# A hybrid block's front stage re-ordered: gate tiles by kind, four of them ahead of the merging of the inverses, spatial gate inside the first chunk, two groups of the recurrence alternating

## The chip, the cores and the metric

The kernel runs on one core of one Trainium2 chip. The metric is the device time of one execution in microseconds (us), here the median of three.

The engines are named as in the profile: PE (TensorE) does the matmuls, PEld its weight loads; DVE (VectorE) and ACT (ScalarE) work elementwise; POOL (GpSimd) and SP (SyncE) only issue transfers here. Every engine runs its own instructions in program order and waits on semaphores (`wait_ge`).

## What is computed

256 tokens, width 1024, fp32. One projection `z = RMSNorm(x) @ W_in` feeds two mixers, which are gated, added and projected out; a top-4-of-32 expert FFN follows.

```python
z_a, u_raw, v_raw, gate_logits = jnp.split(z, ...)
# yA: delta-rule state, 16 heads x 64, over time (in chunks of 64 in the kernel)
sa = einsum('bhij,bhj->bhi', state, -kk_t)
state = state * w_t + sa * (kk_t * a_t) + v_t * k_t
y_t = einsum('bhij,bhj->bhi', state, r_t)
# yB: inside 128-frame chunks
s = einsum('gij,bcjgd->bcigd', tril(ws), LN(gelu(v_raw))) + b_spatial
y_b = gelu(u_raw) * s
g_a, g_b = split(sigmoid(gate_logits + b_gate), 2)
x = x + (g_a * y_a + g_b * y_b) @ w_out
x = x + moe_ffn(rms_norm(x))      # 32 experts: w_gate_up (1024 x 2048), w_down (1024 x 1024) each
return rms_norm(x)
```

## The kernel before, in words

The order of the work is written out by hand, one program for each engine. The tokens are turned so that features lie on partitions; 256 tokens are the moving operand.

The front stage has these parts, in PE's order:

1. The projections of the recurrence's columns, eight pairs of 64-wide heads at a time (`products`, line 1115, makes the 64x64 blocks of each chunk).
2. The values of the spatial gate, `value_chunk`, into PSUM banks 0 to 3, which ACT empties with a gelu (`v_out`).
3. 24 **gate tiles** (`tile`, line 1178): each is eight 128x128 by 128x256 products of `w_in` with the tokens into one half bank. Eight are `u` (gelu), eight are the merge gate `b` and eight the merge gate `a` (sigmoid). They alternate between banks 0 and 1, so tile t waits until ACT has emptied tile t-2 (`f_out`). Their weights come by SP in 1 MB loads of two tiles.
4. **The inverses.** Each chunk needs the inverse of a 64x64 triangular matrix for each head. DVE inverts the 32x32 diagonal blocks on 128 lanes (31 steps of two instructions, lines 806 to 811) after ACT has sent them through memory into that layout (`scr_a`, `al`). ACT sends the result back through memory (`scr_x`, then four loads into `GB`), DVE turns it (`x1_ready`, line 820), and PE merges the blocks in two passes of 32x32 products: `with_x11` (line 1190) and `with_x22` (line 1198).
5. The **spatial gate**: eight pairs of 128x128 products (`spatial`, line 1206); DVE adds the bias and multiplies (lines 841 to 844).
6. **The recurrence**, four chunks q. It is made of groups of 16 products of 64x64 (for each of the eight c, the two half-partitions hh): `rows_of_values`, `rows_of_state`, `solved`, `state_of_values`, `state_of_solved`, `outputs_of_values`, and in `outputs` one group of the state and one of the solved rows. Between them stand `variances`, `spread_deviation` and, in three gaps for each chunk (`fill`, table `FILL`), the 16 tiles b and a. A tile a comes with `gate_lora` (bank 2).
7. The output projection `project_out` (line 1355), router, and then the experts.

A product of 64x64 uses one quarter of PE's array: half of its rows (the partitions that the operands lie on) and half of its columns (the partitions that the result lies on). In the groups that read the state or the solved rows both are `hrows(hh)`; in the groups that read the values the operands lie on `hrows(1 - hh)`, so their two products use the other two quarters.

The experts' weights come in 384 pieces of 1 MB into a ring of 15. SP issues the first nine when the recurrence's last output is made (`y_done`), five when the output projection is done, one after that, and each further one when PE has read the piece that lay in its slot (`pieces_read`).

## Time and profile before

| | us |
|---|---|
| median of 3 runs (1350.76 to 1353.51) | 1353.29 |
| the profiled execution | 1346.54 |
| its span, first to last instruction | 1344.7 |
| PE / DVE / ACT busy | 1213.1 / 291.1 / 178.0 |
| PE without an instruction ahead of `with_x11` | 13.74 |
| first read of an expert's weights (PE, line 1440) | 398.15 |

PE's busy time counts pipelined matmuls from start to end, so it says that there was work, not that the array was full. The table's last line parts the execution: what lies ahead of it is the front stage, what lies behind it are the experts.

### The profile page before, as it was taken

What the parts mean: (1) busy time and instruction counts of PE and PEld (TensorE: products, weight loads), DVE (VectorE), ACT (ScalarE), POOL (GpSimd) and SP (SyncE); (2) the same over time, 40 slices, a digit from 0 to 9 for tenths busy, and PEclk for the clock granted to TensorE, in tenths of its full rate; (3) what the DMA queues carried; (4) which work ended last, traced back from release to release, by engine and by line L of the source; (5) the groups of instructions that cost most, each with busy time, mean ns of one, the idle gap of its engine ahead of it and who ended that gap; (6) DMA issues with size and microseconds to landing.
All of it is one profiled execution on the core that took longest, in us unless ns stands there. A gap on an engine that the chain in (4) does not pass through costs nothing.

```text
span 1344.7 us, 16177 instructions
## 1 busy us (share of the span) xinstructions
PE 1213.1 (90%) x7129; PEld 548.2 (41%) x7129; DVE 291.1 (22%) x590; ACT 178.0 (13%) x341; POOL 12.2 (1%) x26
## 2 busy tenths in 40 slices
PE   6999996999989999899888889988888998888886
PEld 4788665887443333233222223322222332222221
DVE  1156365223331211121111121211111221111112
ACT  3333202212111100000000000100000000000002
POOL 1000000000000000000000000000000000000000
PEclk9999997999969999999999999999999999999999
DMA  8442663223859999999999999999999999999995
GB/s 233 124 109 61 185 206 87 66 93 111 312 210 356 422 422 420 421 423 421 420 422 422 421 421 421 422 420 421 422 422 421 421 420 422 421 421 421 422 421 230
DMA packets 110268, 448.29 MB, mean 333 GB/s; under 512 B 16870, under 2 KB 55888, under 8 KB 61040
## 3 DMA queue, kind: packets, MB, share of 16 engines
q1 hardware_dynamic: 99888, 440.20, 81.9%
q0 software_dynamic: 1600, 4.86, 1.1%
q10 hardware_dynamic: 8704, 2.12, 0.8%
q8 instruction: 59, 0.97, 0.3%
q14 instruction: 17, 0.14, 0.0%
HBM read 445.06 MB, written 2.10 MB: 333 GB/s over the span
## 4 chain that ended last, share of the span: by engine, by line
DMA 50%; PE 44%; DVE 3%; issue 1%; SPq 1%; ACT 1%; ACTq 0%; DVEq 0%
DMA ring<-w_gate_up 46%; PE ps L1440 11%; PE ps L1087 7%; PE ps L1187 5%; PE ps L1460 4%; PE ps L1429 3%; PE ps L1360 2%; DMA ring<-w_down 2%; PE ps L1175 1%; PE ps L1487 1%; SPq L401 1%; DVE prod L809 1%; DVE xl L811 1%; DMA GB<-scr_x 1%; PE ps L1124 1%
## 5 line engine op out<-in xcount | busy, mean ns | idle before, releaser
L1440 PE MATMUL ps<-ring,xT 128*64 128x512 f32 x2048 | 467.6, 598 | 36.2 <-DMA ring<-w_gate_up 34.8
L1460 PE MATMUL ps<-ring,aT 128*64 128x512 f32 x1024 | 239.7, 600 | 45.3 <-DMA ring<-w_down 45.3
L1440 PEld LDWEIGHTS ps<-ring,xT 128*64 128x64 f32 x2048 | 137.2, 136 | 347.7 <-issue 275.6
L1039 DVE TENSOR_SCALAR gc<-ps 128x512 f32<-128x512 f32 x32 | 22.1, 690 | 678.2 <-PE ps L1440 678.2
L1460 PEld LDWEIGHTS ps<-ring,aT 128*64 128x64 f32 x1024 | 67.6, 136 | 214.4 <-issue 125.6
L1087 PE MATMUL ps<-hT,wbuf 128*128 128x256 f32 (+1 forms) x432 | 99.9, 386 | 2.8 <-DVE hT L719 2.8
L1087 PEld LDWEIGHTS ps<-hT,wbuf 128*128 128x128 f32 (+1 forms) x432 | 81.1, 190 | 18.3 <-issue 3.1
L1187 PE MATMUL ps<-hT,wbuf 128*128 128x256 f32 x384 | 88.5, 389 | 0.0
L1187 PEld LDWEIGHTS ps<-hT,wbuf 128*128 128x128 f32 x384 | 73.3, 194 | 12.2 <-issue 1.8
L686 ACT ACTIVATE sgm<-gc 128x512 f32<-128x512 f32 x32 | 20.2, 630 | 359.9 <-DVE gc L1039 359.9
L1487 PE MATMUL ps<-ysl,oht 64*128 64x512 f32 x256 | 63.6, 615 | 0.7 <-ACT ysl L678 0.7
L678 ACT ACTIVATE ysl<-ps 128x512 f32<-128x512 f32 x32 | 19.1, 597 | 240.9 <-PE ps L1460 240.9
L681 ACT ACTIVATE oht<-ps 128x256 f32<-128x256 f32 x32 | 12.3, 383 | 240.5 <-PE ps L1470 240.5
L1035 DVE COPY xT<-ps 128x512 f32<-128x512 f32 x24 | 16.6, 692 | 89.7 <-PE ps L1429 89.7
L1448 PE MATMUL ps<-bgu,consts 32*64 32x512 f32 x256 | 34.8, 612 | 0.0
L1046 DVE TENSOR_TENSOR acts<-uc,sgm 128x512 f32<-128x512 f32 x32 | 34.1, 1064 | 1.1
L1360 PE MATMUL ps<-wbuf,XM 128*128 128x512 f32 x64 | 30.1, 626 | 2.6 <-issue 2.6
L1487 PEld LDWEIGHTS ps<-ysl,oht 64*128 64x128 f32 x256 | 22.0, 186 | 21.9 <-issue 20.3
L1429 PE MATMUL ps<-oh,h2h 128*128 128x512 f32 x64 | 29.4, 460 | 0.0
L1175 PE MATMUL ps<-wbuf,hT 128*128 128x512 f32 x64 | 28.0, 592 | 0.0
L1429 PE MATMUL ps<-oh,h2l 128*128 128x512 f32 x64 | 26.2, 410 | 0.0
L1429 PEld LDWEIGHTS ps<-oh,h2h 128*128 128x128 f32 x64 | 12.5, 195 | 27.3 <-issue 25.7
(257 smaller groups left out, 713.1 us busy)
## 6 DMA issues: line engine op xcount, KB each, us to landing
ring<-w_gate_up SPq DMA_DIRECT2D x256, 1024.0 KB, 26.7
ring<-w_down SPq DMA_DIRECT2D x128, 1024.0 KB, 26.7
wbuf<-w_in SPq DMA_DIRECT2D x26, 512.0 KB, 4.1
wbuf<-w_in SPq DMA_DIRECT2D x12, 1024.0 KB, 5.6
wbuf<-w_in SPq DMA_DIRECT2D x2, 2048.0 KB, 10.2
wbuf<-w_out SPq DMA_DIRECT2D x8, 512.0 KB, 4.0
xacc<-x SPq DMA_DIRECT2D x2, 512.0 KB, 3.8
out<-xacc SPq DMA_DIRECT2D x2, 512.0 KB, 2.7
```

Source lines behind the costliest of these rows:

```text
L686: act_(sgm[:, :], gc[:, :], ACT.Sigmoid, scale=ALPHA).then_inc(sm["sig_done"], 1)
L1039: V.tensor_scalar(gc[:, :], pairs[:, 0, :], LIMIT, None, ALU.min).then_inc(sm["gc_ready"], 1)
L1046: V.tensor_tensor(acts[:, :].rearrange("q (i r p) -> q i p r", p=P, r=2), by_row(uc), by_row(sgm), MUL).then_inc(sm["act_ready"], 1)
L1087: last = mm(proj_slot(n)[0:w, :], wv[:, k, 0:w], hv[:, k, :], start=k == 0, stop=k == KT - 1)
L1175: last = mm(bank(m_), hv[:, k, tb * P:(tb + 1) * P], wv[:, k, :], start=k == 0, stop=k == KT - 1)
L1187: last = mm(f_slot(t), wv[:, k, P * (t % 2):P * (t % 2) + P], hv[:, k, :], start=k == 0, stop=k == KT - 1, skip_group_check=True)
L1360: last = mm(bank(2 * tb + half_), XM_v[:, k, tb * P:(tb + 1) * P], unit((k + 4) % 8)[:, 512 * half_:512 * half_ + 512], start=k == 0, stop ...
L1429: last = mm(bank(b), src[:, tb * D + k * P:tb * D + (k + 1) * P], oh[:, tb * 512:(tb + 1) * 512], start=n == 0, stop=n == 3)
L1440: last = mm(bank(GU_BANK + q, 0, 512, slice(64 * half, 64 * half + 64)), x_, w[:, D * half + 512 * q:D * half + 512 * (q + 1)], start=k == ...
L1448: mm(bank(GU_BANK + q, 0, 512, slice(64 * half, 64 * half + 64)), ident[r, 32 * q + e:32 * q + e + 1].to_broadcast([32, SLOTS]), bgu[r, HA ...
L1460: last = mm(bank(DN_BANK, 0, 512, slice(64 * half, 64 * half + 64)), aT[:, c0:c0 + SLOTS], w[:, D * r + 512 * half:D * r + 512 * (half + 1 ...
L1487: last = mm(bank(OUT_BANK + 2 * tb + half), oht[e % 2][r, tb * P:(tb + 1) * P], ysl[r, :], start=False, stop=False, skip_group_check=True)
```

## The change

It touches the front stage alone. The same products, transfers and elementwise instructions are made, except that DVE makes the merges of two chunks in halves (four instructions more).

- The gate tiles run in the order u, b, a. Twelve instead of eight stand ahead of the recurrence (`EARLY`): ten ahead of `with_x11` (six before), one between the two mergings, one behind. The first twelve rotate over banks 0 to 3.
- Two of the eight spatial products stand ahead of the recurrence, six in the gaps of its first chunk, with tiles b4 to b7. The eight tiles a fill chunks 1 and 2. Chunk 3 has no tile; the first four products of `project_out` fill its gap.
- `at_once` alternates two groups of the recurrence, c by c: `rows_of_state` with `state_of_values`, `solved` with `outputs_of_values`, the outputs of the state with `rows_of_values`.
- ACT sends the blocks to `al` ahead of its second value gelu, and takes the squares of the layer norm after two u tiles. DVE makes the norm's mean inside the inversion, behind step 12, and waits there for ACT's fourth value gelu. It makes half of the normed values ahead of turning the inverse.
- `merged` is done for the first four c in chunk 2's last gap, and `project_out` waits for what it reads.

```diff
-        f_loads = [U0 + 2 * P * i for i in range(4)]
-        f_tiles = [("u", c) for c in range(KT)]
-        for i in range(4):
-            f_loads += [G0 + D + 2 * P * i, G0 + 2 * P * i]
-            f_tiles += [("b", 2 * i), ("b", 2 * i + 1), ("a", 2 * i), ("a", 2 * i + 1)]
+        f_loads = [c0 + 2 * P * i for c0 in (U0, G0 + D, G0) for i in range(4)]
+        f_tiles = [(kind, c) for kind in "uba" for c in range(KT)]
...
-        FILL = [[2, 1, 1], [2, 1, 1], [2, 1, 1], [2, 2, 0]]
+        EARLY = KT + 4
+        FILL = [["b4 s2 s3 b5", "s4 b6 s5", "s6 b7 s7"], ["a0 a1", "a2", "a3"], ["a4 a5", "a6", "a7"], ["", "", ""]]
...
+        def f_bank(t):
+            return t % 4 if t < EARLY else t % 2
...
-            value_gelu(1)
             act.wait_ge(sm["lanes_st"], 64)
             act.wait_ge(sm["bv_ready"], KT)
             act.dma_start(al[:, :], scr_a.rearrange("l s t -> l (s t)")).then_inc(sm["lanes_ld"], 16)
+            value_gelu(1)
...
+                if s == 12:
+                    dve.wait_ge(sm["v_out"], 4)
+                    link(V.tensor_tensor(small[:, 324:326], small[:, 320:322], small[:, 322:324], ADD))
+                    V.tensor_scalar(small[:, 324:326], small[:, 324:326], -1.0 / D, None, MUL).then_inc(sm["ln_mean"], 2)
...
+            normed_values(0)
+            dve.wait_ge(sm["xt_in"], 64)
+            for lo in (0, HD):
+                V.transpose(xw[lo:lo + 32, :].rearrange("s (q t) -> s q t", q=SYS), GBs[lo:lo + 32, :, 0:32]).then_inc(sm["x1_ready"], 1)
+            gate_work("b", 0)
+            normed_values(1)
             dve.wait_ge(sm["w1_done"], 1)
             V.tensor_copy(xw[96:128, :], ps[96:128, 4 * 512:6 * 512]).then_inc(sm["w1_out"], 1)
...
-            def merged(q):
+            def merged(q, cs):
...
+                if q == NCH - 2:
+                    dve.wait_ge(sm["ga_ready"], KT)
+                    merged(0, FRONT_C)
+                    merged(1, FRONT_C)
                 inverse_deviation(q)
...
             def tile(t):
                 j = t // 2
                 pe.wait_ge(unit_sem("f", j), unit_filled("f", j))
-                if t < 2:
+                earlier = [s for s in range(t) if f_bank(s) == f_bank(t)]
+                if earlier:
+                    pe.wait_ge(sm["f_out"], earlier[-1] + 1)
+                else:
                     pe.wait_ge(sm["v_out"], t + 1)
-                else:
-                    pe.wait_ge(sm["f_out"], t - 1)
...
             def spatial(g):
                 pe.wait_ge(sm["vn_ready"], 2)
                 if g < 2:
-                    pe.wait_ge(sm["v_out"], 3 + g)
+                    pe.wait_ge(sm["f_out"], EARLY)
...
-            for t in range(6):
+            for t in range(KT + 2):
                 tile(t)
             with_x11()
-            tile(6)
+            tile(KT + 2)
             with_x22()
-            tile(7)
-            for g in range(GROUPS):
-                spatial(g)
+            tile(KT + 3)
+            spatial(0)
+            spatial(1)
...
+            def at_once(*groups):
+
+                for c in range(KT):
+                    for one in groups:
+                        for hh in range(2):
+                            one(c, hh)
...
+            last_chunk = NCH - 1
+            at_once(rows_of_values(0))
+            for q in range(NCH):
+                if q == 0:
+                    at_once(state_of_values(q))
+                elif q < last_chunk:
+                    at_once(rows_of_state(q), state_of_values(q))
+                else:
+                    at_once(rows_of_state(q))
+                if q < last_chunk:
+                    fill(q, 0)
+                else:
+                    project_out(0, 0, range(0, 4))
+                if q:
+                    spread_deviation(q - 1)
+                at_once(solved(q), outputs_of_values(q))
+                if q == 0:
+                    at_once(rows_of_values(q + 1))
+                elif q < last_chunk:
+                    at_once(outputs_of_state(q), rows_of_values(q + 1))
+                else:
+                    at_once(outputs_of_state(q))
+                fill(q, 1)
+                if q < last_chunk:
+                    at_once(state_of_solved(q))
+                at_once(outputs_of_solved(q))
+                fill(q, 2)
+                if q < last_chunk:
+                    variances(q)
+
             project_out(0, 0, range(4, KT))
-            spread_deviation(NCH - 1)
-            project_out(0, 1, range(KT))
+            variances(last_chunk)
+            project_out(0, 1, range(0, 6))
+            spread_deviation(last_chunk)
+            project_out(0, 1, range(6, KT))
```

PE around the merging of the inverses. Before: tiles are `ps<-hT,wbuf` (eight products each), the 32x32 products merge, `ps<-wst,vsb` is the spatial gate, `ps<-VC,GK` the recurrence's first group.

```order
L1187 MATMUL ps<-hT,wbuf 128x256 x48
L1195 MATMUL ps<-xw,GB 32x32 x64
L1187 MATMUL ps<-hT,wbuf 128x256 x8
L1203 MATMUL ps<-GB,xw 32x32 x64
L1187 MATMUL ps<-hT,wbuf 128x256 x8
L1213 MATMUL ps<-wst,vsb 128x128 x16
L1256 MATMUL ps<-VC,GK 64x64 x16
```

The same place with the change (its lines are numbered on from those of before, so 1187 is 1214 there, 1213 is 1240):

```order
L1214 MATMUL ps<-hT,wbuf 128x256 x80
L1222 MATMUL ps<-xw,GB 32x32 x64
L1214 MATMUL ps<-hT,wbuf 128x256 x8
L1230 MATMUL ps<-GB,xw 32x32 x64
L1214 MATMUL ps<-hT,wbuf 128x256 x8
L1240 MATMUL ps<-wst,vsb 128x128 x4
L1291 MATMUL ps<-VC,GK 64x64 x16
L1326 MATMUL ps<-VC,BK 64x64 x16
L1214 MATMUL ps<-hT,wbuf 128x256 x8
L1240 MATMUL ps<-wst,vsb 128x128 x4
L1214 MATMUL ps<-hT,wbuf 128x256 x8
```

Six tiles ahead of the first merging became ten, and 12 of the 16 spatial products went behind the recurrence's first two groups.

PE in chunk 1 of the recurrence, from its first group to the middle. Before: `ps<-zs,AR` is `rows_of_state`, `ps<-sg,gu` the gate's lora, `ps<-dg,consts` `spread_deviation`, `ps<-rb,GB` `solved`, then the three groups of values.

```order
L1263 MATMUL ps<-zs_111,AR 64x64 x16
L1187 MATMUL ps<-hT,wbuf 128x256 x16
L1324 MATMUL ps<-dg,consts 128x512
L1273 MATMUL ps<-rb,GB 64x64 x16
L1256 MATMUL ps<-VC,GK 64x64 x16
L1282 MATMUL ps<-VC,BK 64x64 x16
L1299 MATMUL ps<-GK,VC 64x64 x16
```

With the change, from the last c of the first alternation on:

```order
L1301 MATMUL ps<-zs_111,AR 64x64 x2
L1326 MATMUL ps<-VC,BK 64x64 x2
L1251 MATMUL ps<-sg,gu_106 128x256
L1252 MATMUL ps<-sg,gu_107 128x256
L1214 MATMUL ps<-hT,wbuf 128x256 x16
L1251 MATMUL ps<-sg,gu_106 128x256
L1252 MATMUL ps<-sg,gu_107 128x256
L1383 MATMUL ps<-dg,consts 128x512
L1314 MATMUL ps<-rb,GB 64x64 x2
L1349 MATMUL ps<-GK,VC 64x64 x2
L1314 MATMUL ps<-rb,GB 64x64 x2
L1349 MATMUL ps<-GK,VC 64x64 x2
```

`rows_of_state` now alternates with `state_of_values` (`ps<-VC,BK`) two by two, and `solved` with `outputs_of_values` (`ps<-GK,VC`), eight times each; the tiles between them are a0 and a1 with a lora each.

DVE between the inversion's last steps and the copies of the merging. Before:

```order
L811 TENSOR_TENSOR xl<-xl,prod 128x31
L815 TENSOR_TENSOR small<-small 128x2
L816 TENSOR_SCALAR small<-small 128x2
L820 STREAM_TRANSPOSE xw<-GB 32x1024 x2
L829 RECIPROCAL small<-small 128x2
L824 TENSOR_SCALAR vsb<-vsb,small 128x1024
L825 TENSOR_TENSOR vsb<-vsb,lng 128x1024
L826 TENSOR_TENSOR vsb<-vsb,lnb 128x1024
L833 COPY xw<-ps 32x1024
```

With the change:

```order
L813 TENSOR_TENSOR xl<-xl,prod 128x31
L861 RECIPROCAL small<-small 128x2
L825 TENSOR_SCALAR vsb<-vsb,small 128x1024
L826 TENSOR_TENSOR vsb<-vsb,lng 128x1024
L827 TENSOR_TENSOR vsb<-vsb,lnb 128x1024
L866 STREAM_TRANSPOSE xw<-GB 32x1024 x2
L842 TENSOR_TENSOR mb<-mb,sgb_120 128x256
L825 TENSOR_SCALAR vsb<-vsb,small 128x1024
L826 TENSOR_TENSOR vsb<-vsb,lng 128x1024
L827 TENSOR_TENSOR vsb<-vsb,lnb 128x1024
L870 COPY xw<-ps 32x1024
```

The turning of the inverse (`xw<-GB`) went behind the first three instructions of the normed values (`vsb`), and the copy of the first merging (`xw<-ps`) has one gate more ahead of it.

## Rows read from the trace of the kernel before

**Rows 1.** The page's first line.

```profile
span 1344.7 us, 16177 instructions
```

**Rows 2.** The page's part 4, the chain that ended last, by line.

```profile
DMA ring<-w_gate_up 46%; PE ps L1440 11%; PE ps L1087 7%; PE ps L1187 5%; PE ps L1460 4%; PE ps L1429 3%; PE ps L1360 2%; DMA ring<-w_down 2%; PE ps L1175 1%; PE ps L1487 1%; SPq L401 1%; DVE prod L809 1%; DVE xl L811 1%; DMA GB<-scr_x 1%; PE ps L1124 1%
```

**Rows 3.** Timeline of SP's queue: start, length, issues of one kind.

```profile
333.78 66.60 SPq L401 DMA_DIRECT2D ring<-w_gate_up  x16
```

**Rows 4.** Busy time in windows, experts' stage: engines, PEclk, DMA share, GB/s.

```profile
1100.00:1300.00 200.00, 174.52 (x794) 52.45 (x794) 24.25 (x42) 14.47 (x26) 0.00 (x0) 1.00 1.01 421
```

**Rows 5.** Chain in order of time, 190 to 240 us: start, length, what.

```profile
192.57 6.16 DMA scr_x<-xl
...
200.37 9.94 DMA GB<-scr_x
...
211.60 1.25 DVE xw L820
...
212.89 3.62 PE ps L1195 x128
216.51 5.65 PE ps L1187 x16
222.16 2.14 PE ps L1203 x128
224.31 3.65 PE ps L1187 x16
...
234.52 1.08 PE ps L1256 x32
```

**Rows 6.** Busy time in windows, as in rows 4, front stage.

```profile
199.10:212.90 13.80, 0.06 (x3) 0.01 (x2) 2.50 (x3) 5.99 (x9) 0.96 (x2) 0.66 0.75 165
...
234.50:258.90 24.40, 24.40 (x329) 20.65 (x330) 5.37 (x13) 6.14 (x9) 0.00 (x0) 1.00 0.17 47
...
336.40:340.00 3.60, 3.60 (x5) 1.54 (x6) 0.49 (x1) 0.00 (x0) 1.52 (x4) 0.53 1.00 371
```

**Rows 7.** Timeline of PE: start, busy, instructions of one line.

```profile
154.01 1.10 PE L1124 MATMUL ps<-AR,bf 64*64 64x128 f32 x32
...
178.27 20.88 PE L1187 MATMUL ps<-hT,wbuf 128*128 128x256 f32 x96
...
243.50 0.22 PE L1256 MATMUL ps<-VC,GK 64*64 64x64 f32 x1
243.50 0.22 PE L1273 MATMUL ps<-rb,GB 64*64 64x64 f32 x1
```

**Rows 8.** Chain in order of time, the recurrence and what follows.

```profile
244.54 0.93 PE ps L1282 x32
...
247.66 3.65 PE ps L1187 x16
...
333.74 2.65 issue
336.39 5.37 PE ps L1360 x8
...
342.78 3.63 PE ps L1360 x8
...
398.15 1.86 PE ps L1440 x7
```

**Rows 9.** Timelines of DVE and ACT.

```profile
178.52 0.42 DVE L809 TENSOR_TENSOR prod<-xl,al 128x252 f32<-128x252 f32 x1
...
327.76 0.42 DVE L853 TENSOR_TENSOR GA<-ps,sga 128x256 f32<-128x256 f32 x1 [5.47 <-ACT sga L579]
...
333.54 0.69 DVE L889 TENSOR_TENSOR yn<-yn,GA 128x512 f32<-128x512 f32 x1
...
178.96 0.19 ACT L566 ACTIVATION_READ_ACCUMULATOR vsb<-ps 128x1 f32 x1
...
204.26 0.38 ACT L570 ACTIVATE mb<-ps 128x256 f32<-128x256 f32 x1 [10.91 <-issue]
```

255 lines of the change are left out of this document (132 added, 123 removed).

## The prediction

> **What bounds the kernel now.** I read the page first. By lines, the chain that ended last is DMA of expert weights for 46% [rows 2]. In the windows of the experts' stage the DMA engines are full (share 1.01, 421 GB/s) and PE is not [rows 4]. So the experts run at the weight stream's rate, and the change can't touch that rate. What it can move is the stream's start. SP's queue shows how: 16 issues of pieces stretch from 333.78 over 66.6 us, to 400.4 [rows 3]. The ring holds 15, so the sixteenth had to wait until PE had read the first, which it began at 398.15 [rows 8]; until then the stream stands still. Whatever the front stage gains on the way to that read should come off the end one for one.
>
> The chain in order of time then says what the front stage waits for. From 192.57 it is not PE: the inverse's blocks go to memory (6.16 us), come back (9.94 us after the last of four loads is issued), and DVE turns them in two instructions, the second at 211.60 [rows 5]. PE has nothing to do for 13.8 us [rows 6]. From 212.89 on PE itself is the chain up to 333.74 [rows 5, 8], without idle time in the chunk that I show [rows 6]. There the length of the recurrence is the sum of PE's instructions, so work taken out or made denser counts.
>
> **The change part by part.**
>
> *Four tiles ahead of the merging.* Six tiles took 20.88 us, 3.48 each [rows 7]. Ten from 178.27 end at 213.1. They don't stall on banks: four banks let tile 8 start once u4 is emptied and tile 9 once u5 is, and ACT, held by its four load issues, goes on with a u tile at 204.26 [rows 9], against 209.6 when tile 9 starts. The four cost 3.65 each where they stood alone in the recurrence [rows 8], somewhat less in pairs; I take 3.6, so 14.4 us leave the path behind the merging.
>
> *The inverse comes later.* Three things bear on `x1_ready`, on which PE started at 212.89 [rows 5]. (a) `al` is asked for earlier, but DVE now waits inside its inversion for ACT's fourth value gelu, whose accumulator is read from 178.96 for 0.19 us [rows 9]. With the two small instructions behind it, step 13 starts near 179.6; it started at 178.52 [rows 9]. The early start is lost in that wait and the chain is 1.0 late. Everything behind on DVE is queued behind it, and `scr_x` waits for the last step. (b) Tiles now run on, so SP's 1 MB load of b6 and b7 is issued at 206, while the blocks come back. It has 1 MB of work for engines that move 421 GB/s at best: between 0 and 2.5 us. I take 0.6, since most of the blocks are ahead of it. (c) Normed values stand ahead of the turning, but their inputs are ready near 208 (tile 7 ends at 206.1, then ACT has u7 and a root with its table), and three instructions of 1024 columns take 3.3 to 4.1 (L889 has 0.69 for 512 columns [rows 9]), about as long as (a) and (b) give; 0.4. Sum 2.0: the merging starts at 214.9 instead of 212.89. Net of the two items 14.4 - 2.0 = **12.4 us**, with 14.4 and 9.5 as ends.
>
> *The clock.* In the 13.8 us without work the granted clock fell (0.66 over that window) [rows 6]. So the first 128 32x32 records took 3.62 us and the tile behind them 5.65, where the second 128 took 2.14 and the next tile 3.65 [rows 5]. That is 1.5 + 2.0 = 3.5 us at the level of 1.2 GHz in place of 2.4. With a wait of some 2 us instead, I count **3.5 us** as gained. The other end is 2.0 (the merging slow, the tile not), from a case in this trace: after only 2.65 us without work the clock was at 0.53 [rows 6, 8].
>
> *Two groups alternating.* Twenty-eight groups of 32 records stand in the recurrence; one costs 0.93 us behind another [rows 8]. Do two groups on different quarters of the array run side by side? Line 1124 is already written so, its four successive products using all four quarters: 32 records of 128 columns took 1.10 us [rows 7]. A group of 64 columns has half the columns to stream and takes about as long, on two quarters. And where `solved` and the next group of values meet, records of both start at the same 243.50 [rows 7]. So I take a pair as 0.98 instead of 1.86. Eight pairs arise (one in each of four chunks, two more in each of chunks 1 and 2): 8 x 0.88 = **7.0 us**. If nothing ran side by side it would be 0; below that, 1 us lost, if each pair paid 0.1 for changing quarters.
>
> The Trainium skill speaks against this in "TensorE: Matmul & The Clock Gate", Part 1: start-to-start of small matmuls never drops below about 25 ns. By that a pair of 64 records would take 1.6 us, eight pairs would save 2.1 us, and the sum below would be 20.5. The trace disagrees with it: 128 records of 32x32 in 2.14 us are 17 ns each [rows 5].
>
> *Spatial gates.* From the end of the tile at 224.31 + 3.65 to the recurrence's first group at 234.52 they took 6.6 us [rows 5], PE and DVE in turn. Now the products hide DVE's part, but PE waits twice: for the sigmoid of b3 ahead of gate 0 (0.6), and for DVE's gate 7 ahead of `variances(0)`, which uses its bank (1.4: sigmoid, then three multiplies and an add at 0.42 each, as L853). I count **0**, between -1.5 and +1.5.
>
> *The end of the recurrence.* Before, PE waited 2.65 us for the merges, and eight records of `project_out` then took 5.37 instead of 3.63 [rows 8]: 4.4 us. Now PE waits where chunk 3's gap begins, for gate a7 (four instructions, 1.7 by L853) and four half merges of 0.42, less the 2.1 of `variances` and `rows_of_state` meanwhile: 1.3. It waits again 0.6 ahead of k = 4, four half merges behind a copy of 0.69 [rows 9]. Later steps are covered: `spread_deviation(3)` has six products as cover. So **2.5 us**, with 0 and 4.4 as ends.
>
> Nothing late is exposed behind it: the output is made some 18 us earlier, so the first nine pieces also go out 18 us earlier; that is enough, since they now have some 57 us until the first read, and 9 MB take 22 at 421 GB/s. The loads of the router and the biases are queued on POOL behind the same event and move with it.
>
> Sum: 12.4 + 3.5 + 7.0 + 0 + 2.5 = **25.4 us**. Span 1344.7 [rows 1] becomes 1319.3, the profiled execution 1346.54 becomes 1321.1. That one is 6.75 us below the median of the runs, a difference that I can't assign; the gain lies ahead of the weight stream, so I carry it over unchanged: 1353.3 - 25.4 = **1328**.
>
> **The rivals.**
>
> *A. The groups don't run side by side.* The hardware might only mix at the border of two long groups, and alternating by two could break this. For it: 32 records took nearly the same time with 64 and with 128 columns, which a limit per weight load would also give. Against it: the common starts at 243.50. The gain is then 18.4, less up to 1: 1335 to 1336. 17%.
>
> *A2. Each start has a floor.* The 32x32 records stand 17 ns apart [rows 5], those of a group 0.93 / 32 = 29 ns [rows 8]. If every start needed something between, a pair would take 1.1 to 1.86 us: gain 24.7 to 18.4, half way 1332. It decides against my term from 20 ns on. For it: no row has 64x64 records of four quarters closer than that over a whole group. Against it: again the common starts. 4%. The skill's rule above is this rival with 25 ns, and gives 1333.
>
> *B. The inverse comes later still.* If b6's load goes wholly ahead of the blocks and the wait of about 4 us drops the clock, 2 us and 3.5 - 2.0 = 1.5 us more are lost, perhaps twice the latter if the tile behind is slow too: gain 20 to 22, 1331 to 1333. For it: DMA was at share 0.75 even averaged over the gap [rows 6]. 14%.
>
> *C. The stream follows only part of it.* If the stream were bound from its first piece, the end would follow `y_done`, 18 us earlier, and not the first read: 1335. Against it: the standstill before the first read [rows 3]. If in addition the recurrence shows new waits, 1338 to 1345. 5%.
>
> *D. Slower, by the clock.* Waits of 0.6 to 2 us now stand at four places. If they kept PE at 1.2 GHz through the recurrence, work would take up to 3.62 / 2.14 = 1.7 or 5.65 / 3.65 = 1.55 times as long [rows 5]. It decides from the point where 45 us of work run so (25 / 0.55); over all the 90 us up to the output projection it would be +50 - 25, so 1378. Against it: work without pause ran at 1.00 in the chunk shown [rows 6]. 2%.
>
> **How the numbers follow.** The likeliest case, that every term holds within its ends, has 58% and gives 1325 to 1331, so 1328. A, A2, B, C and D take 17, 4, 14, 5 and 2. The low end joins the better ends of the terms (14.4 + 3.5 + 7.0 + 1.5 + 4.4 = 31, not all at once; I take 30), the high end takes in A with a loss or with B's first part: 1323 to 1338. A measurement of this kernel can tell about 0.2% from no change, 2.7 us. Only D, and what C could become with more waits, reach that: faster 0.95, same 0.02, slower 0.03.
>
> **What would show it.** In the changed kernel's profile: PE's idle time ahead of the first 32x32 group 1 to 3 us instead of 13.7, those 128 records in 2.1 to 2.3 us; 64 records of an alternating pair in about 1.0 us; the step from the recurrence's first group to the output near 88 us instead of 99; the first read of expert weights near 373. Wrong would be: a pair at 1.9 us (then A), blocks landing after 214 (B), a first read at 373 with an end that moved less (C), or windows of the recurrence granted well under 1.00 (D).

## The result, and the profile of the changed kernel

The changed kernel takes 1334.93 us (median of 4 runs, 1332.11 to 1337.33), beside 1352.03 us for the kernel before (4 runs, 1348.14 to 1353.51). The ratio is 0.9877, 95% interval 0.9847 to 0.9908. I had forecast 1328 and a range of 1323 to 1338: the direction and the range held, but the gain is 17 us, not 25.4.

The page's first line, where [rows 1] had 1344.7:

```profile
span 1335.5 us, 16193 instructions
```

I part both executions at six events. The stages start at: the first gate tile; the first 32x32 product; the recurrence's first group; the issue of the first expert piece (the output is made); the first turning of tokens behind the output projection; the first read of an expert's weights. "Before" stands twice, since I took a second profile of it (below); so does the changed kernel.

| stage, us | before | before, again | forecast | after | after, again |
|---|---|---|---|---|---|
| start to first gate tile | 178.27 | 181.85 | 178.3 | 181.61 | 180.18 |
| to the first merging | 34.62 | 36.45 | 36.6 | 38.28 | 37.88 |
| to the recurrence | 21.56 | 21.17 | 13.4 | 16.57 | 16.57 |
| to the output | 99.29 | 99.29 | 88 | 90.75 | 90.74 |
| to the first turning | 27.10 | 26.99 | 19.7 | 19.79 | 19.79 |
| to the first expert read | 37.24 | 37.11 | 37.2 | 41.44 | 41.44 |
| to the end | 946.65 | 947.57 | 946.7 | 947.08 | 948.64 |

The forecast column is worked out from the prediction: the stage of before less its terms (36.6 is 34.62 + 2.0; 13.4 is 21.56 less 3.5 and less 4.7 for the spatial work that went elsewhere; 19.7 is 27.1 less the 7.4 by which the read was to gain more than the output). Three stages miss: the one behind the merging by 3.2, the recurrence by 2.7, the router's by 4.2.

PE's timeline around the merging, as [rows 5, 7] of before: start, busy, instructions, in brackets the idle time ahead and what ended it.

```profile
219.90 2.84 PE L1222 MATMUL ps<-xw,GB 32*32 32x32 f32 x128 [3.59 <-DVE xw L866]
222.67 6.29 PE L1214 MATMUL ps<-hT,wbuf 128*128 128x256 f32 x16
228.89 2.21 PE L1230 MATMUL ps<-GB,xw 32*32 32x32 f32 x128
231.03 3.72 PE L1214 MATMUL ps<-hT,wbuf 128*128 128x256 f32 x16
235.41 1.13 PE L1240 MATMUL ps<-wst,vsb 128*128 128x128 f32 x8 [0.66 <-ACT sgb L577]
```

The wait fell from 13.74 us to 3.59. But the tile behind the first merging still takes 6.29 us where the next one takes 3.72. The chain in order of time says what came late; compare [rows 5]:

```profile
196.95 6.43 DMA scr_x<-xl
...
207.97 9.35 DMA GB<-scr_x
217.34 1.23 DVE xw L866
```

The inverse's blocks came back at 217.32, seven us later than before (210.31). 3.3 us of that is the later start of the whole front stage.

Busy time in windows (PE, PEld, DVE, ACT, POOL, then PEclk, DMA share, GB/s): behind the first merging, behind `variances(0)`, in the router's part at both ends, and with the experts.

```profile
219.90:228.90 9.00, 9.00 (x146) 7.49 (x146) 5.23 (x6) 1.01 (x1) 0.00 (x0) 0.62 0.15 51
261.13:266.00 4.87, 4.87 (x101) 3.77 (x101) 0.90 (x2) 2.12 (x3) 0.00 (x0) 0.65 0.58 196
...
349.20:362.00 12.80, 12.62 (x34) 6.65 (x34) 3.94 (x13) 1.05 (x1) 0.00 (x0) 0.73 0.55 228
364.00:388.40 24.40, 19.89 (x54) 12.72 (x54) 10.51 (x35) 4.21 (x6) 0.00 (x0) 0.51 0.59 249
1100.00:1300.00 200.00, 174.40 (x796) 52.79 (x794) 20.75 (x36) 14.82 (x27) 0.00 (x0) 1.00 1.01 421
```

So PE worked at the lower of its two levels (1.2 GHz) in three places that I had forecast at 2.4: the first three windows. The fourth, the end of the router's part, was at that level in the kernel before too (the last table of the experiments). The last window is the weight stream, unchanged from [rows 4].

The alternation, in PE's timeline in chunk 3 (`solved` is L1314, `outputs_of_values` L1349):

```profile
323.96 0.23 PE L1314 MATMUL ps<-rb,GB 64*64 64x64 f32 x2
323.98 0.22 PE L1349 MATMUL ps<-GK,VC 64*64 64x64 f32 x2
324.02 0.22 PE L1314 MATMUL ps<-rb,GB 64*64 64x64 f32 x2
...
324.78 0.23 PE L1314 MATMUL ps<-rb,GB 64*64 64x64 f32 x2
324.79 0.23 PE L1349 MATMUL ps<-GK,VC 64*64 64x64 f32 x2
```

Four records start every 58 ns, 14.5 ns each on average, and the 64 of the pair take about 0.95 us, which is what I forecast (0.98). What a pair saves up to the start of the next group is less than that suggests; experiment 2 shows it.

### The profile page after: what moved, and what is told of

It reads as the page before. It is cut to its first block, busy times and chain, and to the rows that moved or that the text cites. A ratio compares the mean times of both kernels' runs of the same rounds, so it can differ in the third digit from the quotient of the medians.

```text
span 1335.5 us, 16193 instructions
## 1 busy us (share of the span) xinstructions
PE 1211.0 (91%) x7129; PEld 544.6 (41%) x7129; DVE 291.3 (22%) x594; ACT 173.9 (13%) x338; POOL 12.2 (1%) x26
## 4 chain that ended last, share of the span: by engine, by line
DMA 50%; PE 44%; DVE 2%; SPq 1%; issue 1%; ACT 1%; ACTq 0%; DVEq 0%
DMA ring<-w_gate_up 46%; PE ps L1516 11%; PE ps L1113 7%; PE ps L1536 4%; PE ps L1214 4%; PE ps L1505 3%; PE ps L1407 2%; DMA ring<-w_down 2%; PE ps L1201 2%; PE ps L1563 1%; SPq L401 1%; DMA GB<-scr_x 1%; DMA consts<-cst 1%; PE ps L1150 1%; PE ps L1524 1%
## 5 line engine op out<-in xcount | busy, mean ns | idle before, releaser
L1061 DVE COPY xT<-ps 128x512 f32<-128x512 f32 x24 | 16.6, 692 | 89.7 <-PE ps L1505 89.7
L1505 PEld LDWEIGHTS ps<-oh,h2h 128*128 128x128 f32 x64 | 12.5, 195 | 27.3 <-issue 25.7
## 6 DMA issues: line engine op xcount, KB each, us to landing
wbuf<-w_in SPq DMA_DIRECT2D x2, 2048.0 KB, 10.9
```

Of the source, the lines that this page charges most:

```text
L1505: last = mm(bank(b), src[:, tb * D + k * P:tb * D + (k + 1) * P], oh[:, tb * 512:(tb + 1) * 512], start=n == 0, stop=n == 3)
```

## The experiments

The kernel before ran beside each group of them: 1350.2 us beside the first four, 1350.8 beside the next four, 1353.5 beside numbers 9 to 11, 1350.9 beside the last.

**1. The changed kernel again.**

> The changed kernel unaltered, for a second profile. Theory (the changed kernel's profile lost 3.3 us at a late start of the first projection and 4.2 us at low clock behind the output projection, both by chance of that execution): here tile 0 starts 1 to 4 us earlier than 181.6, and the stretch from the output projection's third quarter to the first expert read is nearer to the 37.2 us of before than to 41.3. Rival (both come from the change): the two stretches repeat within 0.5 us. Both expect a ratio to before of 0.985 to 0.990.

Measured: 1334.83 us (1331.94 to 1338.34), ratio 0.9874 [0.9848, 0.9900]. The first gate tile started at 180.18, and the table above shows the rest: it repeats to 0.02 us in the stages from the merging to the first expert read, the 41.44 us of the router's part among them. I had called that stage's 4.2 us chance of one execution, and they came again in the second. But both profiled executions (1337.33 and 1337.13 us) are from the slower half of this kernel's eight. On record for each run is the mean granted clock of the whole execution: 0.983 and 0.981 in these two, and 0.987 in three of the four faster runs (1331.94 to 1333.96 us; the fourth, 1332.11, has 0.982). That points to less time at the lower clock in those three. So the stages of the two profiles are hardly those of every execution, and they show the kernel 2.4 us slower than its median.

**2. Without the alternation.** The groups of a pair run one after the other.

```diff
-                for c in range(KT):
-                    for one in groups:
+                for one in groups:
+                    for c in range(KT):
```

> The changed kernel with its groups one behind the other again. Theory (four quarters work side by side, eight pairs save about 0.8 us each): 6 to 7 us slower than the changed kernel, a pair of 64 records 1.9 us instead of 1.1. Rival (the gain of the recurrence comes from its waits and its tiles alone): 0 to 1.5 us slower. The groups' durations in the profile decide, since 6 us is 0.45% of the time.

Measured: 1340.78 us (1338.39 to 1342.31), ratio 0.9920 [0.9904, 0.9937]: 5.95 us slower than the changed kernel. The recurrence takes 101.3 us instead of 90.7, the router's part 37.1 instead of 41.4. In the recurrence two low stretches are part of the difference. Windows of this kernel:

```profile
261.00:269.00 8.00, 8.00 (x57) 5.85 (x54) 0.54 (x1) 1.88 (x2) 0.00 (x0) 0.57 0.12 41
323.00:331.00 8.00, 7.46 (x10) 2.91 (x10) 1.23 (x3) 0.00 (x0) 0.00 (x0) 0.59 0.20 81
```

Summed over windows of 1 us, 12.9 us of PE's work in its recurrence ran at the lower clock, 3.4 us in that of the changed kernel. What the alternation itself gives is read from groups at the higher level. This is the pair of `solved` and `outputs_of_values` in chunk 1, with the start of the group behind it, in the changed kernel:

```profile
275.13 0.27 PE L1314 MATMUL ps<-rb,GB 64*64 64x64 f32 x2
...
276.41 0.27 PE L1358 MATMUL ps<-AR,zs 64*64 64x64 f32 x2
```

and without the alternation:

```profile
275.62 0.97 PE L1314 MATMUL ps<-rb,GB 64*64 64x64 f32 x26
...
277.60 0.97 PE L1358 MATMUL ps<-AR,zs 64*64 64x64 f32 x26
```

That is 1.28 us instead of 1.98 (1.27 in the second profile), the same in chunks 2 and 3; the pair in chunk 0 takes 0.99 instead of 1.74, the outputs of the state with `rows_of_values` 1.09 instead of 1.84 (chunks 1 and 2), and the pair of `rows_of_state` in chunk 2, with the `variances` ahead of it, 2.02 instead of 2.77. With the same 0.75 for that pair in chunk 1, which ran at the lower clock, the eight pairs add up to 5.9 us; the medians differ by 5.95. The other 4.7 us of the recurrence's 10.6 are then the clock's, half of the 9.5 us by which the low work differs.

The two kernels have the same wait of 1.72 us in chunk 3. Here (PE's timeline):

```profile
323.54 6.68 PE L1407 MATMUL ps<-wbuf,XM 128*128 128x512 f32 x8 [1.72 <-issue]
```

and in the changed kernel (chain):

```profile
317.67 1.72 issue
319.40 3.67 PE ps L1407 x8
```

The same wait brought the low clock in one kernel and not in the other. In the router's part it is the reverse: the same records of `project_out` and of the router's weights take 7.11 and 1.97 us without the alternation,

```profile
357.03 1.97 PE L1464 MATMUL ps<-wr,mT 128*128 128x32 f32 x16
358.83 7.11 PE L1407 MATMUL ps<-wbuf,XM 128*128 128x512 f32 x16
```

and in the changed kernel 9.95 and 2.53, behind the same wait of 1.17 us:

```profile
349.22 0.40 PE L1462 MATMUL ps<-br,consts 1*128 1x32 f32 x2 [1.17 <-ACT mT L641]
349.55 2.53 PE L1464 MATMUL ps<-wr,mT 128*128 128x32 f32 x16
351.89 9.95 PE L1407 MATMUL ps<-wbuf,XM 128*128 128x512 f32 x16
```

**3. The four tiles behind the merging.** Tiles b0 to b3, with their sigmoids and gates, stand behind `with_x22`.

```diff
-            for t in range(KT + 2):
+            for t in range(KT):
                 tile(t)
             with_x11()
-            tile(KT + 2)
             with_x22()
-            tile(KT + 3)
+            for t in range(KT, EARLY):
+                tile(t)
```

> The changed kernel with tiles b0 to b3 behind the second merging, with their sigmoids and multiplies, and no tile between the mergings. Theory (the four tiles are hidden in the inverses' way through memory, and keep the clock up): PE waits about 10 us ahead of the first merging (13.7 before, less the two u tiles there, plus 3.6 for the later inverse), the 128 records behind it take 3.6 us, and it is 11 to 16 us slower than the changed kernel, about as slow as before less the alternation. Rival (the stretch is bound by the inverses' chain and the copies, the tiles' place matters little): under 5 us slower.

Measured: 1346.56 us (1345.1 to 1347.92), ratio 0.9969 [0.9956, 0.9982], so 11.7 us slower than the changed kernel. Its wait is

```profile
218.51 3.63 PE L1218 MATMUL ps<-xw,GB 32*32 32x32 f32 x128 [10.59 <-DVE xw L864]
```

and the step from the first merging to the recurrence is 25.8 us instead of 16.6. Of the four tiles, b0 and b1 stood ahead of the first merging, b2 between the mergings and b3 behind them already; so the run prices two hidden tiles, and PE's wait is longer by just these two (10.59 instead of 3.59). The rest of the 11.7 us is the clock, with 9.7 us of low work behind the merging instead of 6.8 and 10.2 instead of 3.4 in the recurrence, and a wait of 1.33 us ahead of the second merging, less 2.5 us in the router's part, which takes 38.9 here.

**4. The later loads held.** SP asks for the weights of b2 and b3 only when the blocks have arrived in memory, and for those of b4 and b5 (and POOL for the gate's lora) only when they are back.

```diff
+                if j == 5:
+                    sp.wait_ge(sm["x_st"], 16)
+                if j == 6:
+                    sp.wait_ge(sm["xt_in"], 64)
...
-            pool.wait_ge(sm["x_st"], 16)
+            pool.wait_ge(sm["xt_in"], 64)
```

> The changed kernel with SP's load of b2, b3 held until the inverses' blocks are stored, that of b4, b5 (and b6, b7 behind it) until they are back, and the load of g_up on POOL too. Theory (the blocks' way back, 13.9 us from the first load's issue, is long because 2.7 MB of other loads share the DMA engines): the way back takes 5 to 9 us, PE waits under 0.5 us ahead of the first merging, its 128 records take 2.2 us, and the time is 5 to 7 us below the changed kernel's (3.6 us of wait, 3 us of low clock). Rival (the way back is bound by its own 128-byte packets and its issues): the way back stays above 12 us and nothing is gained.

Measured: 1327.43 us (1326.52 to 1331.0), ratio 0.9829 [0.9810, 0.9848]: 7.4 us faster than the changed kernel. The page's part on DMA issues (engine, count, KB each, median us from issue to landing) in this stretch of the changed kernel,

```profile
scr_x<-xl ACTq DMA_DIRECT2D x1, 512.0 KB, 6.4
GB<-scr_x ACTq DMA_DIRECT2D x4, 128.0 KB, 8.5
```

and of this one:

```profile
scr_x<-xl ACTq DMA_DIRECT2D x1, 512.0 KB, 2.7
GB<-scr_x ACTq DMA_DIRECT2D x4, 128.0 KB, 7.4
```

From the issue of `scr_x` to the last block back it is 12.4 us instead of 20.4; it was 17.7 and 18.5 in the two profiles of before. The blocks are the same 512 KB each way in all of them. The Trainium skill says in "DMA: Bandwidth & Descriptors", section "Issuing engines are not separate DMA queues", that transfers of all issuing engines run on the same 16 DMA engines and interleave; the trace agrees, with these 8 us. Yet the merging came only 2.4 us earlier after the first gate tile (35.85 instead of 38.28), since now something else ended last. Its chain:

```profile
209.82 1.28 ACT L616
...
211.65 0.82 DVE vsb L829
...
214.98 1.14 DVE xw L870
216.15 1.25 DVE xw L870
217.44 2.21 PE ps L1226 x128
```

The blocks lie there from 209.31 on, but DVE turns them (L870) behind the normed values (`vsb`), and these wait for ACT's root. The wait is 1.15 us, and no low clock follows it (2.21 and 3.72 us for the records and the tile). So most of this kernel's gain is the clock again: the profiles have 2.4 us less up to the merging, 2.8 in the stage behind it, 1.5 in the recurrence and 2.6 in the router's part, and the last two have the same waits as in the changed kernel.

**5. The mean later.** DVE waits for the fourth value gelu behind step 18 of the inversion.

```diff
-                if s == 12:
+                if s == 18:
```

> The changed kernel with DVE's wait for the fourth value gelu (and the mean's two instructions) behind step 18 of the inversion instead of step 12. In the changed kernel DVE stood still for 2.65 us there. Theory (the mis-sized term is the inverse's lateness, and this wait is 2.65 us of it): behind step 18 the gelu is long done, scr_x goes out 2.6 us earlier, the last block lands 2 to 2.6 us earlier, PE's wait ahead of the first merging falls from 3.6 to 1.0 to 1.6 us, and the time is 1332.2 us, or down to 1329 if the low clock behind that wait goes as well. Rival (the transfers decide it, the wait only moves the blocks against other loads): the blocks, issued earlier, meet more of the loads of b4 to b7, land less than 1 us earlier, and the time is 1334 to 1335 us.

Measured: 1328.86 us (1327.72 to 1329.76), ratio 0.9831 [0.9800, 0.9863], the theory's lower number, with the low clock behind the merging gone. DVE had stood still where I forecast a wait. DVE's timeline of the changed kernel:

```profile
182.60 0.16 DVE L820 TENSOR_TENSOR small<-small 128x2 f32<-128x2 f32 x1 [2.65 <-ACT vsb L566]
```

That is gone here, and the inversion ends 2.7 us earlier. But `scr_x` goes out only 1.3 us earlier, because on ACT its issue is queued behind the gelu of u3, which waits for PE. The last step on DVE,

```profile
192.46 0.21 DVE L813 TENSOR_TENSOR xl<-xl,prod 128x31 f32<-128x31 f32 x1
```

and then ACT:

```profile
194.04 0.38 ACT L570 ACTIVATE mb<-ps 128x256 f32<-128x256 f32 x1 [3.01 <-PE ps L1214]
194.05 0.40 ACTq L603 DMA_DIRECT2D scr_x<-xl  x1
```

The last block is back 18.1 us after the issue of `scr_x` instead of 20.4 (no run shows why the way is shorter), the wait ahead of the merging is 1.15 us, and the stage behind it is 13.4 us instead of 16.6. Most of the gain is the clock again. In chunk 3 the low clock came here as well, with 5.37 us for the eight records of `project_out` behind the wait of 1.72 us, where the changed kernel has 3.67.

**6. Gate 7 first.** The last spatial product of chunk 0 ahead of tile b7.

```diff
-"s6 b7 s7"
+"s6 s7 b7"
```

> The changed kernel with the last gap of chunk 0 in the order s6 s7 b7 instead of s6 b7 s7: tile b7 now stands between the last spatial product and the variances that need its bank. Theory (the 1.47 us of waiting for DVE's gate 7 ahead of the variances of chunk 0, and the low clock of 0.64 behind it, are both due to that order): no wait there, a pair of rows_of_state and state_of_values in 1.1 us instead of 1.8 in chunk 1, the first group of the recurrence to the output 2.5 to 3.5 us shorter (87.5 instead of 90.7), time 1331.8 us. Rival (the wait only moves, since DVE's gate 7 needs the sigmoid and four elementwise instructions whatever is ahead): 89 to 90.7 us for that stretch, time 1333.5 to 1335 us. In both the stretch from the first turning of the tokens behind the output projection to the first read of expert weights stays 41.4 or goes to 37.1 to 38.9 us, which moves the time by up to 4 us on top: that part the stage's length tells apart, not the time.

Measured: 1333.39 us (1328.74 to 1334.22), ratio 0.9870 [0.9838, 0.9901]. The wait of 1.47 us and the low clock behind it are gone, but the low clock came at 311 to 315 instead, behind the wait in chunk 3. The recurrence took 89.1 us, the lower end of what the rival expected: the wait itself could be removed, but the clock's part of it moved. The median is 1.4 us below the changed kernel's, which is no difference clear of the noise.

**7. The inverse turned first, loads held.**

```diff
-            normed_values(0)
             dve.wait_ge(sm["xt_in"], 64)
...
+            normed_values(0)
             gate_work("b", 0)
```

> The kernel with the loads of the later tiles held back until the blocks are back (1327.4 us), and in it DVE turns the inverse ahead of the normed values, as in the kernel before. There the blocks were back at 209.3 but the first merging began at 217.44, since DVE worked on the normed values until 214.9 behind ACT's root. Theory (with the loads held, the order on DVE is what ends last, by 1.0 us over PE's ten tiles): turned inverse ready at 211.9, the merging starts when the tenth tile ends, 216.4 to 216.5, without a wait; 1326.4 us. Rival (the normed values or the copies of the merging become late in turn): a wait of 1 us or more ahead of the second merging or the first spatial product, time 1327.4 us or more.

Measured: 1332.36 us (1328.46 to 1335.27), ratio 0.9867 [0.9832, 0.9902]. In the trace the mechanism is as expected, the merging starts without a wait:

```profile
214.00 2.21 PE L1226 MATMUL ps<-xw,GB 32*32 32x32 f32 x128
```

1.2 us sooner after the first gate tile than in experiment 4; a wait of 0.50 us ahead of the second merging takes 0.4 of it back. But the median is 4.9 us above that kernel's. The profiled run (1328.46) had 41.5 us in the router's part instead of 38.8, with some 7 us of low work between the two turnings where experiment 4 has 3.4. Its two slowest runs (1333.88 and 1335.27) have a mean granted clock of 0.981 and 0.982, the other two 0.985 and 0.986, which points to more low work in the slowest two; where, isn't in any trace.

**8. All four edits of 4 to 7.**

> All four edits at once: loads held, inverse turned ahead of the normed values, mean behind step 18, and s6 s7 b7. Theory (each wait of the changed kernel has its own cause and the gains add, except that the mean's earlier step has nothing left to give once the blocks are back ahead of the tenth tile): 1334.8 - 7.4 (held) - 1.0 (turned first) - 3.0 (s6 s7 b7) = 1323.4 us, with no wait over 0.3 us ahead of the first merging. Rival (the low clock is not a matter of these waits but comes back elsewhere, above all in the stretch behind the output projection, 41.4 us in two executions of the changed kernel and 37.1 to 38.9 in the three variants): 1326 to 1328 us.

Measured: 1326.09 us (1324.63 to 1327.76), ratio 0.9814 [0.9781, 0.9847]. No wait ahead of the merging, yet the rival's time: the low clock came behind the wait of 1.72 us in chunk 3, as in experiments 2, 3, 5 and 6. Windows there and in the router's part:

```profile
306.60:315.00 8.40, 6.68 (x11) 2.90 (x10) 2.23 (x6) 0.60 (x1) 0.00 (x0) 0.59 0.30 121
355.00:376.00 21.00, 18.33 (x52) 11.32 (x50) 8.53 (x31) 2.40 (x3) 0.00 (x0) 0.51 0.57 240
```

**9. The wait filled.** Seven products of constants ahead of `with_x11`; their result is never read.

```diff
+            def busy(b, n):
+                for _ in range(n):
+                    mm(bank(b, 0, 256), C("ones"), C("carry"), start=True, stop=True)
...
+                busy(4, 7)
                 pe.wait_ge(sm["x1_ready"], 2)
```

> The changed kernel with seven products of constants (128x256, result never read) on PE in the wait ahead of the first merging; no wait, transfer or order of anything else is changed. In the changed kernel PE stands still there for 3.6 us, and then works at a granted clock of about 0.5 up to 229. Theory (the low clock follows from PE's standing still): no low clock behind the first merging; the 128 records take 2.0 to 2.2 us instead of 2.6 to 2.8 and the tile behind them 3.65 instead of 6.22, so the first recurrence group comes 3.2 us sooner after the first merging (13.4 instead of 16.57), and the time is 1331.6 us. Rival (the clock falls for another reason, such as the kind of work or the transfers): 16.6 us for that stretch and 1334 to 1335 us. The low clock in later places may shift and move the time by some 2 us either way in both cases; the stretch decides.

Measured: 1331.57 us (1327.45 to 1332.54), ratio 0.9835 [0.9804, 0.9865]. In its timeline (L1219 are the added products)

```profile
215.46 3.19 PE L1219 MATMUL ps<-consts 128*128 128x256 f32 x14
220.07 2.21 PE L1227 MATMUL ps<-xw,GB 32*32 32x32 f32 x128 [1.43 <-DVE xw L866]
222.22 3.72 PE L1214 MATMUL ps<-hT,wbuf 128*128 128x256 f32 x16
```

the records and the tile behind them have their full speed, and the stage is 13.37 us instead of 16.57, though the merging itself starts no earlier (39.14 us after the first gate tile, 38.28 before the filling). That was the theory's number, to 0.03 us: PE's standing still was the cause there, and not the transfers or the kind of work. The profile has more than the expected 3.2 us: the recurrence takes 89.3 us and the router's part 38.9, 1.5 and 2.5 less than in the changed kernel, though their waits are the same. That the median fell by 3.3 us only fits the changed kernel's profiles being slower than its median.

**10. All four edits, and the other waits filled too.** `busy(1, 3)` ahead of the output projection in chunk 3, `busy(7, 2)` ahead of both groups of router logits, `busy(5, 8)` ahead of the second turning of tokens, `busy(5, 3)` ahead of the second down bias.

> The kernel with all four edits (1326.1 us), and products of constants in PE's waits ahead of the output projection in chunk 3 (three), ahead of both groups of router logits (two each), ahead of the second turning of tokens (eight) and ahead of the second down bias (three). They are as long as the waits are. Theory (these waits bring the low clock that stood from 307 to 315 and from 355 to 376): both stretches at the higher level; recurrence to output 88 us instead of 90.6, second turning to the first read of expert weights 14 us instead of 21.7, and the time is 1326.1 - 2.6 - 8 = 1315.5 us. Rival (dependent short steps bound the router's part, PE's clock hardly counts): that part 19 us or more, time 1321 to 1324 us. Third (extra work only queues ahead of the real one): 1326 us or more.

Measured: **1317.14 us** (1316.02 to 1317.78), ratio 0.9736 [0.9712, 0.9759], the best version, 9 us below experiment 8, or 10.5 by the two ratios. Recurrence to output 87.7 us, first turning to first read 30.7 instead of 37.1 in experiment 8. From the second turning to the first read it is 15.25 us instead of 21.65, where the theory had 14. The same windows as there, the second moved with the stage:

```profile
306.60:315.00 8.40, 8.11 (x115) 4.79 (x117) 3.84 (x10) 0.56 (x1) 0.00 (x0) 1.00 0.29 115
351.30:366.50 15.20, 14.63 (x64) 9.99 (x64) 9.03 (x33) 2.40 (x3) 0.00 (x0) 0.89 0.84 351
```

**11. The kernel before again**, for a second profile.

> The kernel before once more, for a second profile. Theory: its first profile began its front stage early by chance (first gate tile at 178.27, changed kernel and variants 178.9 to 181.6), so here that tile starts 1 to 3 us later, everything from there to the end takes the same 1166.5 us within 2 us, and the run is nearer the median of 1350 to 1352 than 1346.5. Rival: the change itself delays the first gate tile; then it starts at 178.3 again and the span is 1344.7 again.

Measured: 1352.24 us, span 1350.4, first gate tile at 181.85, and 1168.6 us from it to the end (1166.5 in the first profile). So the start differs by 3.6 us between two executions of one kernel. Its chain at the start has

```profile
1.66 8.28 DMA consts<-cst
```

which the first profile's chain doesn't have. What brings that load into the chain no run shows. The changed kernel's front stage didn't start late; the profile that I had read was one with an early start. That explains 3.6 of the 6.75 us by which it lay below its median; another 2.1 came behind the first gate tile.

**12. The kernel before with its waits filled**: `busy(4, 28)` ahead of the first merging, `busy(1, 5)` ahead of the output projection, and the router's part as in experiment 10.

> The kernel before with products of constants in PE's waits: 28 ahead of the first merging, five ahead of the output projection, and in the router's part the same fifteen as in the kernel with all edits. Theory (the low clock in the front stage and in the router's part is a cost of its own, which the change did not take away but which can be had without it): first merging to the recurrence 18.0 us (21.2 to 21.6 before), output to the first turning of tokens 25.4 (27.0), that turning to the first read of expert weights 30.7 (37.1); together 11.5 us off, ratio to the kernel before 0.9915. The change with its four edits and the same filling then still beats it by 24 us, close to the 25.4 that I forecast. Rival (the router's part was short only in the changed order, where the weights arrive at other times): 35 us or more there, and a ratio above 0.995.

Measured: 1342.14 us (1340.4 to 1343.78), ratio 0.9931 [0.9907, 0.9955]. The router's part is 31.7 us instead of 37.1, output to first turning 25.4 instead of 27.0. The stage behind the merging kept 20.9 us, since the filling ended 3.32 us too soon there:

```profile
199.75 12.25 PE L1192 MATMUL ps<-consts 128*128 128x256 f32 x56
215.32 3.62 PE L1200 MATMUL ps<-xw,GB 32*32 32x32 f32 x128 [3.32 <-DVE xw L820]
218.87 5.10 PE L1187 MATMUL ps<-hT,wbuf 128*128 128x256 f32 x16
```

The merging waits for the transfers whether PE works meanwhile or not, but 3.3 us of standing still bring the low clock as 13.7 did. With the waits filled in both, kernel 10 beats this one by 25 us (each was measured beside its own runs of before, whose medians differ by 2.7).

Low work of each kernel from the first gate tile on, summed over windows of 1 us as (1 - PEclk) x 2 x PE's busy time, windows at 0.97 or more left out:

| us of PE's work at the lower clock | before | again | after | 2 | 3 | 4 | 5 | 6 | 7 | 8 | 9 | 10 | 12 |
|---|---|---|---|---|---|---|---|---|---|---|---|---|---|
| up to the second turning | 10.9 | 9.9 | 17.0 | 16.3 | 23.9 | 3.4 | 6.8 | 9.6 | 6.8 | 5.8 | 3.4 | 0 | 6.4 |
| from there to the first expert read | 18.0 | 17.3 | 19.8 | 17.8 | 18.1 | 17.8 | 19.5 | 17.9 | 19.9 | 17.8 | 17.9 | 3.4 | 6.8 |

Between the first turning and the first expert read, the length of the router's part follows its low work (the table's second row and what lies between the two turnings) in every profile: 37.1 to 37.2 us with about 18 us of it, 38.8 to 38.9 with 21.3, 39.6 with 22.9, 41.4 to 41.5 with 26.7, 30.7 with 3.4 and 31.7 with 6.8. Each us of low work costs about half a us, as in the recurrence.

## Why the prediction was right, and where it was off

**The bound.** Right. From the first expert read to the end all profiles have 946.7 to 948.6 us, whether that read begins at 366.5 or at 402.9. What the front stage gains comes off the end one for one; rival C is rejected.

**Four tiles ahead, 14.4 less 2.0.** The 14.4 held as far as the runs show: PE's wait fell from 13.74 to 3.59 us, which is 13.8 us for four tiles less the 3.7 by which the merging came later, and experiment 3, which puts two of them behind the merging, has 7.0 us more of it. The lateness was 3.3 to 3.7 us by the profile that I read, 1.4 to 1.8 by the second one. Part (a), DVE's wait inside the inversion, is there, and `scr_x` goes out 1.0 us later after the first gate tile than in the first profile (15.3 against 14.3), as forecast, but no later than in the second, so that its 1.0 isn't shown; experiment 5 recovered 1.3. Part (b) was mis-sized: 0.6 us for the loads beside the blocks, against 1.5 to 2.6 more in the transfers than before and 8 us less when these loads are held. I asked only which load was new. If holding them would bring the kernel before to the same 12.4 us, its wait of 13.7 us held some 5 us of this contention; no run has tried it. Part (c), 0.4, cost nothing while the blocks were late, and 1.2 once they were early (experiments 4 and 7).

**The clock, 3.5.** The prediction stayed in its range, but this step failed: "with a wait of some 2 us instead, I count 3.5 us as gained". The wait was 3.6 us, and 3.2 of the 3.5 were not gained; filling that wait gained them (experiment 9). Rival B named it and had the place right. And the low clock is not a matter of this place alone. It came behind `variances(0)`, at the router and, in other orders, in chunk 3. In its profiles the changed kernel did more of its front work at 1.2 GHz than the kernel before, 17.0 us against 10.9, where my sum counted on less. This took 1.5 us of the recurrence's gain (89.3 us in experiments 4, 7 and 9, which have no low work there) and 4.2 in the router's part, to which my sum gave nothing at all.

**The alternation, 7.0.** The mechanism is right, the size was 1.1 us too large: 0.95 us for 64 records as forecast, but 5.9 us for the eight pairs and 5.95 in the median (experiment 2). I had set a pair against 1.86 us, two groups at 0.93. Two groups on different quarters already took 1.74, since they mix where they meet; the common starts at 243.50, which I used as evidence, are that mixing. Rivals A and A2 are rejected. The floor of about 25 ns between starts that the Trainium skill gives in "TensorE: Matmul & The Clock Gate", Part 1, does not hold for these products: they start 14.5 ns apart. Part 3 of that page of the Trainium skill says that products on different parts of the array run concurrently, and that is what the trace shows.

**Spatial gates, 0.** The waits came as forecast (0.66 for the sigmoid, 1.47 for gate 7); the low clock behind the second was not in the term.

**The end of the recurrence, 2.5.** Output to first turning is 19.79 us, 7.3 less than before; the new wait of 0.31 us (forecast 0.6) lies inside it. 3.6 of the 7.3 is the part of `project_out` that moved into chunk 3, and 1.72 the new wait there (forecast 1.3). So 2.0 us instead of 2.5, mostly by that longer wait.

**Sum.** From the first gate tile to the end the first profiles of the two kernels differ by 12.5 us (1166.4 and 1153.9), not by 25.4. Off are 1.7 for the inverse's lateness, 3.2 behind the merging, 3.2 in the recurrence, whose terms add up to 87.5 us (1.5 by the clock, 1.1 by the alternation, 0.4 by the wait in chunk 3, 0.2 open), 4.2 at the router and 0.5 in the other stages: 12.8 us, of which 8.9 are the clock's. The medians differ by more, 17.1 and, in experiment 1, 15.4, since both profiles of the changed kernel are slower than its median, and the first one of the kernel before is faster than its own.

That the time fell into the range is in part luck. 1334.93 us is neither in the likeliest case (1325 to 1331) nor at rival B (1331 to 1333), whose mechanism is what the trace shows; it lies beside rival A (1335 to 1336), which is false. The range reached that far for A. Rival D, slower by the clock, is rejected as such: its mechanism is there, in stretches of a few us.

What stays open is what decides where the low clock comes. The same wait of 1.72 us in chunk 3 brought it in experiments 2, 3, 5, 6 and 8, not in the changed kernel nor in 4, 7 and 9; the same 1.17 us at the router brought it in the changed kernel, not in experiment 2. Experiment 9 shows that PE's standing still is a cause, and 10 that filling the waits removes it; no run told the length from which a wait is one. Nor does a trace show why executions of one kernel differ in it, as those of the changed kernel and of experiment 7 do by their mean clocks.

## What to carry to other kernels

When a wait on a bounding TensorE gets shorter but doesn't go, don't count the clock behind it as regained; count the waits that the change adds, and look at PEclk in the next stage, also where the change touches nothing. If a wait can't be removed, products that nobody reads can fill it, and here they were worth 9 us, in the kernel with all edits and in the kernel before. They must reach to the end of the wait: ahead of the merging in experiment 12 they ended 3.3 us too soon and gave next to nothing.

When the chain goes through small transfers, ask what else is in flight on the DMA engines, not only what is new: holding back loads that were not yet needed took 8 us off the round trip. Only 2.4 of them reached the products that waited for it, since the next thing in line ended last. And see what the issue of a transfer is queued behind on its engine, since an earlier producer gains only up to that.

One profile is one execution. Where it lies some us off its median, part it at an event that the change doesn't touch, and compare from there.

## What I had not expected of the chip

- Two groups of 64x64 products on different quarters of the array, alternating by two products, start their records 14.5 ns apart on average, 58 ns for four.
- 15 products of constants (30 records, 8.2 us) brought the router's part from 37.1 to 30.7 us, with PE's low work there down from 17.8 to 3.4 us.
- 512 KB out to memory and back in four pieces of 128 KB took 12.4 to 12.8 us in the four kernels with the other loads held, and 17.7 to 21.3 us beside them.
